# State sums of an SSD scan from split operands, and a group of small products cut in two

## The chip, the core and the metric

The kernel runs on one core of a Trainium2 chip. The time is what the device needs for one execution, in microseconds (us), as the median of several runs. TensorE (PE) multiplies, VectorE (DVE) and ScalarE (ACT) work elementwise, GpSimd (POOL) does small copies, and SyncE (SP) issues the DMAs.

## What is computed

Two layers of a hybrid decoder trunk for 512 prompt tokens and 8 x 8 sample tokens. Each layer projects the normed input to the inputs of three branches: an SSD (Mamba-2) scan of 16 heads, 8 retention heads, and pooling. A second projection takes their outputs back. The change touches two places of it, the sum that updates the SSD state after a chunk, and the product of the sample queries with the retention states. From the reference:

```python
def step(h, inp):                      # SSD, one chunk of 128 tokens
    ...
    y = jnp.einsum('btsg,btsgh,bsghp->btghp', scores, decay, xdt)
    y = y + jnp.einsum('btgn,bghpn->btghp', cc, h) * jnp.exp(cum)[..., None]
    last = cum[:, -1]
    w_end = jnp.exp(last[:, None] - cum)
    h_new = h * jnp.exp(last)[..., None, None] + jnp.einsum('bsgn,bsgh,bsghp->bghpn', bc, w_end, xdt)
...
def step(s, inp):                      # retention
    ...
    y = y + jnp.einsum('bthd,bhde->bthe', qc, s) * inner_decay[None, :, :, None]
```

All of it is in fp32.

## The kernel before

**Units.** A layer is a sequence of 60 units, u = 0 to 59. A unit is one projection of 128 output columns over all 576 tokens: 2 halves of 288 tokens x 8 steps k over the input. Each step is three fp32r products, high weights times high input, high times low, low times high (`products`, L554 to L556), so 48 products a unit. The operands are split for that: ScalarE copies the weights to fp32r (`high`, L942) and VectorE subtracts that copy from them (`split`, L1227), two units ahead. Everything else on TensorE stands between units, in program order, and runs in plain fp32.

**Order.** There is no planner. Each engine has its own loop over u, with the branch work written out by unit number, and semaphores between them. `project(u, between, at)` issues the 48 products and calls `between` after step number `at` (half * 8 + k). The SSD chunks t = 0 to 4 take units 26 to 35, two units a chunk; t = 4 is the sample tokens, and has no state sum. For chunks 0 to 3:

- TensorE, end of the even unit, `ssd_turn(t)`: transposes of x (L662) and B (L667) and the scores product. End of the odd unit, `ssd_y(t)`: first the state sums (L676), one fp32 product of 512 columns per group, then the 16 heads' outputs (L690, with L693 for the old state).
- VectorE, even unit, `ssd_1(t)` (L1380, L1381 makes `xdw`, L1383), the weight split (L1227), then `ssd_weights(t)` (L1392, twice), which multiplies the decays with the scores. Odd unit, `ssd_2(t)`: new state (L1422, L1425) and outputs (L1434), then `c_decay`. In units 28 and 30 a pooling chain (L1588 on) stands behind `ssd_weights`.
- ScalarE, even unit: the high half of the weights of unit u + 2, half of the decay's clamps (L1033), a copy of turned B to `btok` (L1119), the decay's exponentials (L1040), then the readout of the unit (L986 to L996).

**Waits.** Before L676 TensorE waits for `s_xdt` (`ssd_1`) and `s_bt` (L1119). Only before L690 it waits for `s_M` (`ssd_weights`):

```python
pe.wait_ge(*of(s_bt, t + 1))
if t < TILES - 1:
    for g in range(GROUPS):
        mm = pe.matmul(mb[:, g, :], btok[:, g, :], xdw[:, g * 512:(g + 1) * 512], start=True, stop=True)
    mm.then_inc(s_S, 1)
pe.wait_ge(*of(s_M, t + 1))
```

**Retention.** In unit 22 (`S_RST`) `ret_inter` runs after step 7: 64 fp32 products of 64 x 64 weights and 8 columns, L784, with one signal at the end (`rs_I`) for which VectorE waits in `ret_sample_y` (L1558); `ret_decayed` (L1569) follows there.

Of the kernel before, what the change touches and what calls it, by code (L numbers as in the profile page):

```python
# [8 lines left out]
F32 = mybir.dt.float32  # L9
# [4 lines left out]
P = 128  # L14
# [8 lines left out]
HEADS = 16  # L23
# [106 lines left out]
def trunk(nc: bass.Bass, a):  # L130
    with ExitStack() as ctx:
# [33 lines left out]
        decay = place("decay", [P, 2, HEADS, CH], at=work)  # L165
        cdec_t = place("c_decayed", [P, HEADS, CH], at=work + 4 * 4096)
        xdt = place("xdt", [P, HEADS * HD], at=work + 4 * 6144)
        xdw = place("xdt_to_end", [P, HEADS * HD], at=work + 4 * 7168)
        hT = place("ssm_state", [P, HEADS * HD], at=work + 4 * 8192)

# [18 lines left out]
        two_at = top[0]  # L189
        ssq = place("ssq", [P, TOK])  # L190
        rstd = place("rstd", [P, TOK])
        itok = place("sample_inter_tok", [P, HEADS * HD], at=two_at)
        tab = place("tab", [P, TAB_N])
        vec = place("vec", [P, V_N])
# [12 lines left out]
        gm = place("scores", [P, GROUPS, CH])  # L207
        btok = place("b_tok", [P, GROUPS, P])
        masked = top[0]
        bseq_ = place("b_tok_seq", [P, 2, GROUPS * P])  # L210
        el = place("exp_last", [P, HEADS])
        els = place("exp_last_sample", [P, HEADS, NB])
# [95 lines left out]
        sT = sem("ssd_turned", TILES)  # L308
        s_xdt = sem("ssd_xdt", TILES)
        s_bt = sem("ssd_b_tok", TILES)  # L310
        s_exp = sem("ssd_exps", TILES)
        s_row = sem("ssd_row_exps", TILES - 1)
        s_ec = sem("ssd_c_decayed", TILES - 2)
# [222 lines left out]
        def _(pe):  # L536
# [79 lines left out]
                        mm = products(0, half, k)  # L616
                mm.then_inc(proj, 1)

            def project(u, between=None, at=KT - 1):

                pe.wait_ge(*of(w_split, u + 1))
                o = u - U_OUT
                if u == 1:
                    pe.wait_ge(*of(x_new, 2 * OUT_CHUNKS, l - 1))
                elif o < 2:
                    pe.wait_ge(*of(evac, u - 1))
                else:
                    pe.wait_ge(*of(x_new, o - 1))
                for half in range(2):
                    for k in range(KT):  # L630
                        if half == 0 and u == EARLY:
                            pe.wait_ge(*of(h_lo, k + 1))
                        if half == 0 and o == 0:
                            pe.wait_ge(*of(mix_lo, k + 1))
                        if half == 0 and o == OUT_CHUNKS:
                            pe.wait_ge(*of(y_lo, k + 1))
                        mm = products(u, half, k)
                        if half * KT + k == at and between is not None:
                            between()
                mm.then_inc(proj, 1)  # L640

            def norm_sum(at):
# [27 lines left out]
            def ssd_y(t):  # L670
                n = rows(t)
                pe.wait_ge(*of(s_xdt, t + 1))
                pe.wait_ge(*of(s_bt, t + 1))
                if t < TILES - 1:
                    for g in range(GROUPS):
                        mm = pe.matmul(mb[:, g, :], btok[:, g, :], xdw[:, g * 512:(g + 1) * 512], start=True, stop=True)  # L676
                    mm.then_inc(s_S, 1)
                pe.wait_ge(*of(s_M, t + 1))
                inter = 0 < t < TILES - 1
                if inter:  # L680
                    pe.wait_ge(*of(s_ec, t))
                for j in range(PAIRS):
                    if t < TILES - 1:
                        dst = mb[:, 2 + j // 4, (j % 4) * P:(j % 4) * P + n]
                    else:
                        dst = mb[:, 2, j * SMP:(j + 1) * SMP]
                    for e in range(2):
                        h = 2 * j + e
                        r = slice(e * HD, (e + 1) * HD)
                        mm = pe.matmul(dst[r, :], xdt[0:n, h * HD:(h + 1) * HD], decay[0:n, t % 2, h, 0:n],  # L690
                                       start=True, stop=not inter)
                        if inter:
                            mm = pe.matmul(dst[r, :], hT[:, h * HD:(h + 1) * HD], cdec_t[:, h, :],  # L693
                                           start=False, stop=True)
                mm.then_inc(s_Y, 1)
# [77 lines left out]
                            mm = pe.matmul(mb[r, 1, j * HD:(j + 1) * HD], kw[:, c], vtok[:, c], start=True, stop=True)  # L773
                    mm.then_inc(r_S, 1)

            def ret_inter():

                pe.wait_ge(*of(r0_in, 16))
                for n in range(NB):
                    b = RET_SEQ_OF[n]  # L780
                    for j in range(RP):
                        for e in range(2):
                            r = slice(e * HD, (e + 1) * HD)
                            mm = pe.matmul(mb[r, 3 - e, j * SMP + b * NT:j * SMP + (b + 1) * NT],  # L784
                                           rs0[r, n // STRIPS, n % STRIPS, j, :], qd[r, j, b * NT:(b + 1) * NT],
                                           start=True, stop=True)
                mm.then_inc(rs_I, 1)

            def ret_sums(q):

# [77 lines left out]
            for l in range(DEPTH):  # L868
# [4 lines left out]
                for u in range(1, UNITS if l + 1 < DEPTH else UNITS - 2):  # L873
# [1 line left out]

                        pe.wait_ge(*of(pool_out, u - U_GPOOL - 1))
                    if u == S_RST:
                        project(u, ret_inter)
                    elif S_RST < u <= S_RST + 2:
                        project(u, lambda: ret_sums(u - S_RST - 1))  # L880
                    elif u == S_SST:

                        def beside():
                            pool_mm_(3)
                            ssd_inter(0)

                        project(u, beside)
                    elif u == S_SST + 1:
                        project(u, lambda: ssd_inter(1))
                        ssd_inter_turn()  # L890
                    elif u == S_SST + 2:
                        project(u, lambda: ssd_sums(0, 0))
                    elif u == S_SST + 3:
                        project(u, lambda: ssd_sums(0, 1), 2)
                        ssd_sums(1, 0)
                    elif u == S_SST + 4:
                        project(u, lambda: ssd_sums(1, 1), KT)
                    elif u == S_NORM + 2:
                        project(u, lambda: ssd_norm_sum(0))
                        ssd_norm_sum(1)  # L900
                    elif u == S_RN + 2:
                        project(u, lambda: (ret_norm_sum(2), ret_norm_sum(3)), KT + KT // 2)
                    elif U_GPOOL < u < U_GPOOL + 4 and (u - S_SSD) % 2 == 0:
                        project(u, lambda: pool_mm_(u - U_GPOOL - 1))
                    elif u > 1 or l:
                        project(u)
# [24 lines left out]
        def _(eng):  # L931
# [148 lines left out]
            for l in range(DEPTH):  # L1080
                for u in range(UNITS if l + 1 < DEPTH else UNITS - 2):
# [30 lines left out]
                    if even:  # L1112

                        t = (u - S_SSD) // 2
                        if t > 0:
                            ssd_clamp(t, 1, 2)
                            eng.wait_ge(*of(s_S, t))
                        eng.wait_ge(*of(sT, t + 1))
                        go(act(btok[:, :, :], mb[:, 3, 0:256].rearrange("p (g n) -> p g n", g=2), ACT.Copy),  # L1119
                           s_bt, t + 1)  # L1120
                        if t > 0:
                            ssd_decay(t)
                    if EARLY <= u < U_OUT:
# [32 lines left out]
                        ssd_clamp(0, u - S_RET, 4)  # L1156
                    if u == S_RET + 4:
                        ssd_decay(0)
                    if S_SSD <= u < S_SST - 1 and not even:
                        t = (u - S_SSD) // 2 + 1  # L1160
                        ssd_row_exps(t)
                        ssd_clamp(t, 0, 2)
# [55 lines left out]
        def _(eng):  # L1218
# [154 lines left out]
            def ssd_1(t):  # L1373
                n = rows(t)
                eng.wait_ge(*of(sT, t + 1))
                src = mb[:, 0:2, :].rearrange("p a (h d) -> p (a h) d", d=HD)
                dt_b = tokv[:, t, 32:48].unsqueeze(2).to_broadcast([P, HEADS, HD])
                dw_b = tokv[:, t, 64:80].unsqueeze(2).to_broadcast([P, HEADS, HD])
                settle()
                go(V.tensor_tensor(heads(xdt[:, :]), src, dt_b, ALU.mult))  # L1380
                go(V.tensor_tensor(heads(xdw[:, :]), src, dw_b, ALU.mult))  # L1381
                mask = (T("causal") if t < TILES - 1 else T("smask")[0:SMP, :])
                go(V.tensor_tensor(gm[0:n, :, 0:n], mb[0:n, 2, 0:256].rearrange("p (g n) -> p g n", g=2)[:, :, 0:n],  # L1383
                                   mask.unsqueeze(1).to_broadcast([n, GROUPS, n]), ALU.mult), s_xdt, t + 1)

            def ssd_weights(t):
                n = rows(t)
# [269 lines left out]
            for l in range(DEPTH):  # L1657
                for u in range(UNITS if l + 1 < DEPTH else UNITS - 2):
# [49 lines left out]
                    if S_SSD <= u < S_SST:  # L1708
                        t = (u - S_SSD) // 2
                        (ssd_weights if even else ssd_2)(t)  # L1710
                        if (u - S_SSD) % 2 == 1 and t + 1 < TILES - 1:
                            c_decay(t + 1)
                    if U_CONV <= u < U_POOL:
# [296 lines left out]
```

## Time and profile before

| | us |
|---|---|
| median of 3 runs | 954.91 (954.11 to 955.33) |
| the profiled execution | 958.53 |
| its span, first to last instruction | 956.7 |
| TensorE busy | 945.1 (99%) |
| VectorE busy | 679.9 (71%) |
| ScalarE busy | 423.7 (44%) |
| mean granted TensorE clock | 0.992 |

Read first which engine fills the span, then what it waits for, then its clock by stretches. A TensorE record lasts longer than its turn in the stream, since matmuls are pipelined: the distance between the starts of records is what a product costs. An fp32 product leaves two records, an fp32r product one.

### The profile page before, as it was taken

The page shows a single profiled execution, that of the slowest core. Times are in us where ns is not written, and L with a number is a line of the kernel's source. Part 1 is how long each engine was busy: PE and PEld are TensorE (multiplying, and loading weights), DVE is VectorE, ACT ScalarE, POOL GpSimd, SP SyncE. Part 2 cuts the span into 40 slices and gives each one's busy share as a digit, 9 for nine tenths or more (in the row PEclk, how much of TensorE's full clock was granted, in tenths as well). Part 3 has the DMA queues.
Part 4 walks back from the last instruction along what each step waited for, and adds up shares of the span by engine and source line. Part 5 has one row for each costly group of instructions (what it writes and reads, how often), then busy time and mean ns, then how long its engine had stood idle before and what let it go on. Part 6 is the DMA issues. An engine that isn't in the chain of part 4 may idle for free.

```text
span 956.7 us, 18777 instructions
## 1 busy us (share of the span) xinstructions
PE 945.1 (99%) x7942; PEld 898.9 (94%) x7942; DVE 679.9 (71%) x927; ACT 423.7 (44%) x710; POOL 43.5 (5%) x148
## 2 busy tenths in 40 slices
PE   8999999999999999999999999999999999999996
PEld 7899999999989889999999999999989988999996
DVE  6787778666995568664557877777679747786544
ACT  6432553235774145532334225532267632554243
POOL 0000101010010000000000001101101000000000
PEclk9999999899999999999999999998999999999999
DMA  7334222134234463323432442122433452562222
GB/s 277 105 116 140 69 66 67 51 111 155 91 106 158 152 223 127 131 91 111 132 128 66 135 143 67 46 67 53 159 105 101 138 200 66 221 209 67 76 80 100
DMA packets 38421, 112.56 MB, mean 118 GB/s; under 512 B 11104, under 2 KB 14048, under 8 KB 36928
## 3 DMA queue, kind: packets, MB, share of 16 engines
q1 hardware_dynamic: 38080, 110.46, 35.2%
q8 instruction: 63, 1.03, 0.5%
q0 software_dynamic: 256, 0.88, 0.3%
q14 instruction: 22, 0.18, 0.1%
HBM read 93.85 MB, written 17.47 MB: 116 GB/s over the span
## 4 chain that ended last, share of the span: by engine, by line
PE 90%; DVE 4%; ACT 4%; DMA 1%; issue 1%; SPq 0%; DVEq 0%; ACTq 0%
PE acc L554 26%; PE acc L556 25%; PE acc L555 25%; PE misc L690 1%; ACT decay L1033 1%; PE misc L676 1%; PE misc L743 1%; ACT w_hi L942 1%; PE misc L784 1%; PE misc L765 1%; DVE w_lo L1227 1%; PE acc L833 1%; PE misc L814 1%; ACT decay L1040 1%; PE misc L707 1%; DVE conv_out L1588 1%
## 5 line engine op out<-in xcount | busy, mean ns | idle before, releaser
L554 PE MATMUL acc<-hin,w_hi 128*128 128x288 f32 x1504 | 452.9, 301 | 0.3 <-DVE x L1673 0.3
L556 PE MATMUL acc<-hin,w_lo 128*128 128x288 f32 x1504 | 444.9, 296 | 0.0
L555 PE MATMUL acc<-hin,w_hi 128*128 128x288 f32 x1504 | 444.8, 296 | 0.0
L554 PEld LDWEIGHTS acc<-hin,w_hi 128*128 128x128 f32 x1504 | 284.2, 189 | 12.9 <-issue 11.3
L942 ACT ACTIVATE w_hi<-w_raw 128x1024 fp32r<-128x1024 f32 x119 | 125.8, 1057 | 379.9 <-PE acc L556 378.2
L555 PEld LDWEIGHTS acc<-hin,w_hi 128*128 128x128 f32 x1504 | 284.4, 189 | 0.4
L556 PEld LDWEIGHTS acc<-hin,w_lo 128*128 128x128 f32 x1504 | 284.1, 189 | 0.0
L1227 DVE TENSOR_TENSOR w_lo<-w_raw,w_hi 128x1024 fp32r<-128x1024 f32 x119 | 145.4, 1222 | 135.2 <-ACT w_hi L942 134.9
L554 PE MATMUL acc<-mix,w_hi 128*128 128x288 f32 x416 | 124.3, 299 | 1.3 <-DVE mix L1233 0.9
L556 PE MATMUL acc<-mix,w_lo 128*128 128x288 f32 x416 | 122.6, 295 | 0.0
L555 PE MATMUL acc<-mix,w_hi 128*128 128x288 f32 x416 | 122.5, 294 | 0.0
L554 PEld LDWEIGHTS acc<-mix,w_hi 128*128 128x128 f32 x416 | 78.0, 188 | 4.8 <-issue 3.5
L555 PEld LDWEIGHTS acc<-mix,w_hi 128*128 128x128 f32 x416 | 78.0, 188 | 0.3
L556 PEld LDWEIGHTS acc<-mix,w_lo 128*128 128x128 f32 x416 | 78.0, 188 | 0.0
L1333 DVE SCALAR_TENSOR_TENSOR conv_out<-halo,vec,conv_out 128x600 f32<-128x600 f32 x72 | 60.8, 844 | 2.5
L1033 ACT ACTIVATE decay<-decay,token_vecs 128x128 f32<-128x128 f32 (+1 forms) x160 | 47.8, 379 | 1.9
L1673 DVE TENSOR_TENSOR x<-x,acc 128x576 f32<-128x576 f32 x30 | 22.6, 754 | 28.4 <-PE acc L556 26.4
L946 ACT ACTIVATE mix<-x,vec 128x576 fp32r<-128x576 f32 x16 | 12.0, 770 | 38.7 <-DVE x L1673 34.5
L690 PE MATMUL misc<-decay,xdt 128*64 128x128 f32 (+1 forms) x320 | 27.3, 266 | 0.0
L960 ACT ACTIVATE tmp<-x 128x576 f32<-128x576 f32 x22 | 14.8, 679 | 25.5 <-DVE x L1673 12.2
L690 PEld LDWEIGHTS misc<-decay,xdt 128*64 128x64 f32 (+1 forms) x320 | 19.5, 136 | 6.8 <-issue 6.8
L1380 DVE TENSOR_TENSOR xdt<-misc,token_vecs 128x1024 f32<-128x1024 f32 x10 | 12.2, 1225 | 18.1 <-PE misc L667 17.8
(218 smaller groups left out, 1052.6 us busy)
## 6 DMA issues: line engine op xcount, KB each, us to landing
w_raw<-in_w SPq DMA_DIRECT2D x119, 512.0 KB, 3.7
decay<-cum_rows SPq DMA_DIRECT2D x8, 1024.0 KB, 6.2
h<-in_ssm SPq DMA_DIRECT2D x16, 512.0 KB, 6.7
out_ssm_s<-h SPq DMA_DIRECT2D x16, 512.0 KB, 6.0
x<-in_x SPq DMA_DIRECT2D x8, 576.0 KB, 6.3
x_kept<-x SPq DMA_DIRECT2D x4, 576.0 KB, 2.8
x<-x_kept SPq DMA_DIRECT2D x4, 576.0 KB, 5.8
out_y<-x SPq DMA_DIRECT2D x8, 288.0 KB, 2.3
```

Source lines behind the costliest of these rows:

```text
L554: pe.matmul(out, wh, hi, start=k == 0, stop=False)
L555: pe.matmul(out, wh, lo, start=False, stop=False)
L556: return pe.matmul(out, wl, hi, start=False, stop=k == KT - 1)
L690: mm = pe.matmul(dst[r, :], xdt[0:n, h * HD:(h + 1) * HD], decay[0:n, t % 2, h, 0:n], start=True, stop=not inter)
L942: go(act(w_hi[:, unit % 2, :, :], w_raw[:, unit % RAW, :, :], ACT.Copy), w_hid, unit + 1, 0)
L946: go(act(raw_h(0, j), x[:, j, :], ACT.Copy, scale=vec[:, V_NW + j:V_NW + j + 1]), p_hi, j + 1, at)
L960: go(act(tmp[:, j % 2, :], x[:, j, :], ACT.Square), sqd, j + 1, at)
L1033: go(act(m, m, ACT.Relu, scale=-1.0, bias=tokv[0:n, t, h:h + 1]))
L1227: go(V.tensor_tensor(w_lo[:, unit % 2, :, :], w_raw[:, unit % RAW, :, :], w_hi[:, unit % 2, :, :].bitcast(F32), ALU.subtract), w_split, un ...
L1333: ins = V.scalar_tensor_tensor(out=o, in0=h[:, c:c + CVO], scalar=w[c], in1=o, op0=ALU.mult, op1=ALU.add)
L1380: go(V.tensor_tensor(heads(xdt[:, :]), src, dt_b, ALU.mult))
L1673: go(V.tensor_tensor(halves(x[:, m, :]), halves(x[:, m, :]), acc_of(whole(l, u)), ALU.add), x_new, o + 1)
```

## The change

The state sums of chunks 0 to 3 become three fp32r products per group, from split operands. The high half of turned B is written by the ScalarE copy that made `btok` before, now of type fp32r. The high half of `xdw` is a new ScalarE copy of 1024 elements, behind the readout of the even unit. The low halves are two VectorE subtractions in a new `ssd_low`, called behind `ssd_weights`. TensorE waits for a new semaphore, `s_xlo`, before the sums. Separately, `ret_inter` is cut into two calls of 32 products, after steps 2 and 9 of unit 22; the signal comes after the second.

```diff
@@ ssd_y
                 if t < TILES - 1:
+                    pe.wait_ge(*of(s_xlo, t + 1))
                     for g in range(GROUPS):
-                        mm = pe.matmul(mb[:, g, :], btok[:, g, :], xdw[:, g * 512:(g + 1) * 512], start=True, stop=True)
+                        b, c = slice(g * P, (g + 1) * P), slice(g * 512, (g + 1) * 512)
+                        pe.matmul(mb[:, g, :], btok_2[:, 0, b], xdw_hi[:, c], start=True, stop=False)
+                        pe.matmul(mb[:, g, :], btok_2[:, 0, b], xdw_lo[:, c], start=False, stop=False)
+                        mm = pe.matmul(mb[:, g, :], btok_2[:, 1, b], xdw_hi[:, c], start=False, stop=True)
                     mm.then_inc(s_S, 1)
@@ ret_inter
-            def ret_inter():
+            def ret_inter(part):
 
                 pe.wait_ge(*of(r0_in, 16))
-                for n in range(NB):
+                for n in range(STRIPS * part, STRIPS * (part + 1)):
...
-                mm.then_inc(rs_I, 1)
+                if part:
+                    mm.then_inc(rs_I, 1)
@@ TensorE's loop
                     if u == S_RST:
-                        project(u, ret_inter)
+                        project(u, lambda: ret_inter(0), 2, lambda: ret_inter(1), KT + 1)
@@ ScalarE's loop
-                        go(act(btok[:, :, :], mb[:, 3, 0:256].rearrange("p (g n) -> p g n", g=2), ACT.Copy),
-                           s_bt, t + 1)
+                        if t < TILES - 1:
+                            go(act(btok_2[:, 0, :], mb[:, 3, 0:256], ACT.Copy), s_bt, t + 1)
+                        else:
+                            go(act(btok[:, :, :], mb[:, 3, 0:256].rearrange("p (g n) -> p g n", g=2), ACT.Copy),
+                               s_bt, t + 1)
...
+                    if even and t < TILES - 1:
+                        eng.wait_ge(*of(s_xdt, t + 1))
+                        go(act(xdw_hi[:, :], xdw[:, :], ACT.Copy), s_xhi, t + 1)
@@ VectorE
+            def ssd_low(t):
+
+                eng.wait_ge(*of(s_bt, t + 1))
+                go(V.tensor_tensor(btok_2[:, 1, :], mb[:, 3, 0:256], btok_2[:, 0, :].bitcast(F32), ALU.subtract))
+                eng.wait_ge(*of(s_xhi, t + 1))
+                settle()
+                go(V.tensor_tensor(xdw_lo[:, :], xdw[:, :], xdw_hi[:, :].bitcast(F32), ALU.subtract), s_xlo, t + 1)
...
                         (ssd_weights if even else ssd_2)(t)
+                        if even and t < TILES - 1:
+                            ssd_low(t)
```

The new tiles lie in memory that is free in those units: `xdw_lo` over `xdw` itself, `xdw_hi` over the norm's two work tiles, `btok_2` over `b_tok_seq`.

## Rows read from the trace of the kernel before

**Rows 1.** The page: busy time of the engines.
```profile
PE 945.1 (99%) x7942; PEld 898.9 (94%) x7942; DVE 679.9 (71%) x927; ACT 423.7 (44%) x710; POOL 43.5 (5%) x148
```

**Rows 2.** Waits of TensorE, the longest: in total us, times, longest us.
```profile
PE misc L867 <- DVE pad_eps L1640: 1.7, 1, 1.7
```

**Rows 3.** TensorE by windows: us, busy (records), clock, DMA share, GB/s.
```profile
180.00:190.00 10.00, 10.00 (x152) 0.66 0.19 61
...
183.00:184.00 1.00, 1.00 (x26) 0.54 0.00 0
...
650.00:651.00 1.00, 1.00 (x36) 0.85 0.06 13
```

**Rows 4.** TensorE's timeline at the retention products: start, duration, then the instruction.
```profile
179.67 0.29 PE L555 MATMUL acc<-hin,w_hi 128*128 128x288 f32 x1
179.80 0.29 PE L556 MATMUL acc<-hin,w_lo 128*128 128x288 f32 x1
180.03 4.50 PE L784 MATMUL misc<-q_decayed,ret 64*64 64x8 f32 x128
...
184.86 0.44 PE L555 MATMUL acc<-hin,w_hi 128*128 128x288 f32 x1
185.10 0.44 PE L556 MATMUL acc<-hin,w_lo 128*128 128x288 f32 x1
...
647.94 4.75 PE L784 MATMUL misc<-q_decayed,ret 64*64 64x8 f32 x128
```

**Rows 5.** TensorE's timeline at the state sums of chunk 0: all four records, then the last alone.
```profile
226.18 1.88 PE L676 MATMUL misc<-xdt_to_end,b_tok 128*128 128x512 f32 x4
...
227.47 0.59 PE L676 MATMUL misc<-xdt_to_end,b_tok 128*128 128x512 f32 x1
```

**Rows 6.** VectorE's timeline in the unit before them.
```profile
222.30 0.41 DVE L1383 TENSOR_TENSOR scores<-misc,tab 128x256 f32<-128x256 f32 x1
222.63 1.22 DVE L1227 TENSOR_TENSOR w_lo<-w_raw,w_hi 128x1024 fp32r<-128x1024 f32 x1
223.95 2.36 DVE L1392 TENSOR_TENSOR decay<-decay,scores 128x1024 f32<-128x1024 f32 x2
```

**Rows 7.** Timeline of all engines at chunk 1, some lines.
```profile
242.45 2.36 DVE L1392 TENSOR_TENSOR decay<-decay,scores 128x1024 f32<-128x1024 f32 x2 [0.56 <-ACT decay L1040]
...
243.73 0.65 ACT L991 ACTIVATE qk<-acc 128x576 f32<-128x576 f32 x1
244.12 0.32 PEld L676 LDWEIGHTS misc<-xdt_to_end,b_tok 128*128 128x128 f32 x2
244.24 1.88 PE L676 MATMUL misc<-xdt_to_end,b_tok 128*128 128x512 f32 x4
244.50 1.06 ACT L942 ACTIVATE w_hi<-w_raw 128x1024 fp32r<-128x1024 f32 x1
```

**Rows 8.** The same view at chunk 3.
```profile
282.31 2.36 DVE L1392 TENSOR_TENSOR decay<-decay,scores 128x1024 f32<-128x1024 f32 x2
283.48 0.65 ACT L996 ACTIVATE tmp<-acc 128x576 f32<-128x576 f32 x1
...
285.32 1.88 PE L676 MATMUL misc<-xdt_to_end,b_tok 128*128 128x512 f32 x4
```

**Rows 9.** The same view at chunk 1 of the second layer.
```profile
711.65 0.65 ACT L991 ACTIVATE qk<-acc 128x576 f32<-128x576 f32 x1
...
712.16 1.88 PE L676 MATMUL misc<-xdt_to_end,b_tok 128*128 128x512 f32 x4
```

**Rows 10.** VectorE behind the retention products; VectorE and TensorE at the turn of chunk 3.
```profile
191.53 1.22 DVE L1227 TENSOR_TENSOR w_lo<-w_raw,w_hi 128x1024 fp32r<-128x1024 f32 x1 [3.70 <-ACT w_hi L942]
...
273.67 2.16 DVE L1434 SCALAR_TENSOR_TENSOR xbc<-xbc,vec,misc 128x128 f32<-128x128 f32 x8
...
276.08 1.03 PE L662 MATMUL misc<-tab,xbc 128*128 128x128 f32 x8
```

**Rows 11.** TensorE by windows, behind its last product.
```profile
951.10:954.40 3.30, 0.00 (x0) 1.00 0.87 307
```

More of the change, by code:

```diff
@@ L167, in trunk @@
         xdt = place("xdt", [P, HEADS * HD], at=work + 4 * 6144)
+        xdw_lo = place("xdt_to_end_low", [P, HEADS * HD], F32R, at=work + 4 * 7168)
         xdw = place("xdt_to_end", [P, HEADS * HD], at=work + 4 * 7168)
@@ L191, in trunk @@
         rstd = place("rstd", [P, TOK])
+        xdw_hi = place("xdt_to_end_high", [P, HEADS * HD], F32R, at=two_at)
         itok = place("sample_inter_tok", [P, HEADS * HD], at=two_at)
@@ L209, in trunk @@
         masked = top[0]
+        btok_2 = place("b_tok_high_low", [P, 2, GROUPS * P], F32R, at=masked)
         bseq_ = place("b_tok_seq", [P, 2, GROUPS * P])
@@ L310, in trunk @@
         s_bt = sem("ssd_b_tok", TILES)
+        s_xhi = sem("ssd_to_end_high", TILES - 1)
+        s_xlo = sem("ssd_to_end_split", TILES - 1)
         s_exp = sem("ssd_exps", TILES)
@@ L617, in project_again, with project @@
                 mm.then_inc(proj, 1)
-            def project(u, between=None, at=KT - 1):
+            def project(u, between=None, at=KT - 1, then=None, then_at=KT):
                 pe.wait_ge(*of(w_split, u + 1))
@@ L639, in project @@
                             between()
+                        if half * KT + k == then_at and then is not None:
+                            then()
                 mm.then_inc(proj, 1)
```

## The prediction

> **What bounds the kernel now.** I read the page first: TensorE is busy for 945.1 us, 99% of the span [rows 1]. Then the waits of TensorE: the longest is 1.7 us, at the start, and all others are under 1 us, none of them in chunk work [rows 2]. So TensorE bounds every stage, and whatever TensorE does or waits for is on the path that sets the end. Third, its clock by stretches: the mean is 0.66 in 180 to 190 us. Windows of 1 us show where it goes from the higher of its two levels (1.00, 2.4 GHz) to the lower (0.50, 1.2 GHz): 0.54 in 183 to 184 us is a fall at 183.1, and in the second layer 0.85 in 650 to 651 us is one at 650.7 [rows 3]. The two layers show nothing else of the kind. What TensorE did before each fall is the timeline's: 128 records of 8 columns (the retention sample products) for 4.5 us [rows 4]. Last, for each chunk, when TensorE reaches the state sums and when VectorE and ScalarE are done [rows 5 to 9]: VectorE is closer to being late than the busy shares tell.
>
> **Part 1, the state sums on TensorE (L676).** Now one chunk takes two fp32 products, in four records. The first starts at 226.18, the fourth at 227.47, so they follow each other every 1.29 / 3 = 0.43 us, 1.72 us in all [rows 5]. Afterwards there are six fp32r products of 512 columns; the trace has none of that size. The fp32r products of 288 columns come every 0.13 us (a whole unit of 48 gives 0.133), and every 0.24 at the low clock [rows 4]. 0.24 us for 288 columns at 1.2 GHz is one column a cycle, so at 2.4 GHz a product is 0.120 plus 0.013 us. With a fixed extra, 512 columns take 0.213 + 0.013 = 0.226, six take 1.36; in proportion 0.236, six take 1.42. I take the first: the extra is absent at the low clock, where the columns take twice as long, so it doesn't look proportional. Gain per chunk 0.36 (0.30) us, times 8 chunks (4 in each of 2 layers): **-2.9 us** (-2.4). A loss is excluded: it would need 0.29 a product, over twice the 288-column row. The change of tile shape on the way to L690 stays as it is. The records show two records for an fp32 product, each of 0.43 us for 512 columns, two cycles of 2.4 GHz a column, so four in all. The Trainium skill ("FP8 and Floating Point Precision", section TensorE Precision Notes) says that true FP32 takes four passes; the trace agrees. The skill's "TensorE: Matmul & The Clock Gate" (section Back-to-back issue gap) has 2.5 ns over the columns' time where the rows have 13; by it, as an estimate, six would take 1.30 us and the gain be 3.4 us; the rows decide.
>
> **Part 2, what TensorE now waits for.** The sums need both halves of the split. ScalarE copies the high half (1024 elements a partition) after its readout; VectorE subtracts twice, and *after* its two score products (L1392). Until now the scores were needed only at L690, 1.8 us after TensorE reached the sums. That cover is taken away, and two more VectorE instructions are put before the same point. Prices: the subtraction of 1024 has a twin, L1227, 1.22 us; the one of 256 from PSUM is like L1383, 0.41 (it follows at 0.33) [rows 6]; the copy of 1024 is like L942, 1.06 us [rows 7]. A released engine starts 0.05 us later, and a product starts 0.12 us after its weight load [rows 7]; between independent instructions of ScalarE or VectorE lies an overlap of about 0.09 us [rows 6, 7].
> Chunk 0: scores end 223.95 + 2.36 = 226.31; small subtraction to 226.64; large one 226.68 to 227.90; TensorE starts at 228.07 instead of 226.18 [rows 5, 6]: wait 1.89 us. The copy is done earlier: ScalarE only reads out in this unit.
> Chunk 1: here ScalarE is last. Its Silu readout ends at 243.73 + 0.65 = 244.38, the copy runs 244.29 to 245.35, the large subtraction 245.40 to 246.62, TensorE starts 246.79 instead of 244.24: 2.55 us [rows 7]. (On VectorE alone, with scores to 244.81, it would be some 0.4 less.)
> Chunk 2 repeats chunk 1, with the same operations at the same distances: 2.55 us.
> Chunk 3: a pool product (L833) makes TensorE arrive later. Silu from 283.48, copy to 285.10, subtraction to 286.37, start 286.54 instead of 285.32: 1.22 us [rows 8].
> Together 8.21 us a layer. Layer 2 has the same distances (Silu 711.65, arrival 712.16, against 243.73 and 244.24) [rows 7, 9]: **+16.4 us**. Lower bound, VectorE alone, small subtraction 0.33, no refill of the array: about 1.6 + 2.0 + 2.0 + 0.6 = 6.2 a layer, 12.4. Upper bound, 0.3 us more for each chunk in handing over: 18.8.
> Queued behind the new instructions: on VectorE the pool chains of chunks 1 and 2, the next weight split and the state update (L1434 ends 273.67 + 2.16 = 275.83, just before TensorE's turn of chunk 3 at 276.08) [rows 10]. It shifts by some 1.7 us, TensorE by 2.55 - 0.36 = 2.2, so its margin grows from 0.25 to about 0.7: no second wait. On ScalarE the next high half of the weights comes up to 0.9 us later, and TensorE isn't there either. Cost of both: 0.
>
> **Part 3, the retention products in two parts.** If the clock stays up, the low stretches go. Layer 1: the mean of 0.66 means 0.34 / 0.5 x 10 = 6.8 us at the low level, from 183.1 to 189.9. From 184.5, where the small products end, one product comes every 0.24 instead of 0.133 us: 5.4 / 0.24 = 22.5 products, 2.4 us. In the 1.4 us before, the small products themselves ran slower, x26 in 183 to 184 against the mean of 128 / 4.4 = 29, about 0.45 us [rows 3, 4]. In layer 2 the fall comes 0.3 us earlier in the group and the group is 0.25 us longer; I take the same 2.85 us. Together **-5.7 us**. Cost: one more change of tile shape into and out of the small products, about 0.1 us each way (as 179.80 to 180.03 where 0.13 is usual) [rows 4]: +0.4 us. The products end some 0.9 us later, at index 9 instead of 7 of the unit, and what VectorE does behind them is followed by an idle of 3.70 us [rows 10]: 0.
>
> **Sum.** 16.4 - 2.9 - 5.7 + 0.4 = +8.2 us. The profiled execution took 958.53 us, 1.8 over its span: it would become 966.7. It lies 3.6 above the median of 954.91, and my forecast is for the median: **963.1 us**.
>
> **Rivals.** *B, the clock falls in the new waits.* Before, TensorE had no pause over 1.7 us in its stream. A pause of 2.5 us, four of them in 8 chunks, could send it to the low level, where it stayed 6.8 us [rows 3]. That costs 6.8 x (1 - 0.133 / 0.24) = 3.0 us for each fall; one to four falls give 966.1 to 975. Against it: behind its last product TensorE did nothing from 951.1 to 954.4, and the clock was still at 1.00 [rows 11]. For it: it fell although TensorE was never idle [rows 3, 4]. The Trainium skill (the clock page above, section Why this matters for your kernels) blames drops on idle gaps between bursts; the two falls here had no gap, so the trace shows that it takes less, and the page's rule gives this rival, not the forecast.
> *C, the split doesn't hold the clock.* Each part still has 64 records, nearly 2 us of work that hardly fills the array. If both layers still fall, the 5.7 us stay: 968.8. For the split speaks that both falls came 2.8 to 3.1 us after the start of the group (183.1 against 180.03, 650.7 against 647.94) [rows 3, 4], longer than a part.
> *D, faster.* The gains of 8.2 us win if the eight waits sum to less than 8.2, 1.0 us each. That happens if the work ahead of the sums is shorter by half: since the scores alone end 0.13 us (chunk 0) and 0.57 us (chunk 1) after TensorE's arrival and 0.65 before it (chunk 3) [rows 5 to 8], what comes behind them would have to cost 0.6 us instead of 1.6. With free subtractions the waits would be some 0.3 + 0.7 + 0.7 us a layer, 3.4 in all, and the time 954.9 + 3.4 - 8.2 = 950.1. Against it stands the twin instruction at 1.22 us.
>
> **How the numbers follow.** Forecast 50%, B 27%, C 13%, D 5%, and 5% for times just around the kernel before. The forecast's own bounds: 954.9 + 12.4 - 2.9 - 5.8 + 0.2 = 958.8, and 954.9 + 18.8 - 2.4 - 5.5 + 0.6 = 966.4. The range has to take in C and up to two or three falls of B: 958.5 to 971. A measurement can tell about 0.2% (1.9 us) from no change. Slower 92%, same 4%, faster 4%.
>
> **What would show it.** A row "L676-line products <- VectorE xdt_to_end" among TensorE's waits, 16 us in 8 times, 1.9, 2.5, 2.5 and 1.2 long; fp32r products of 512 columns every 0.226 us; the clock at 1.00 in the small products, now in two groups of some 1.9 us; L1434 and the turns without a wait. Wrong would be: waits of half that length (then D), a clock of 0.5 behind the sums (B) or in the retention unit (C), or a wait at the turn of chunk 3.

## The result and the profile after

| | us |
|---|---|
| before, median | 955.12 |
| after, median | 972.63 (971.29 to 973.40) |
| ratio | 1.0172, 95% interval 1.0150 to 1.0193 |
| profiled execution after, and its span | 973.24, 971.5 |
| before, profiled execution and span | 958.53, 956.7 |

The change makes the kernel 17.5 us slower, by the profiled executions 14.7 us. I had forecast 8.2 us, and the range ended at 971.

The waits of TensorE in the kernel after (in total us, times, longest us), which answer [rows 2]:

```profile
PE misc L685 <- DVE xdt_to_end_low L1410: 14.9, 8, 2.3
PE misc L879 <- DVE pad_eps L1666: 1.7, 1, 1.7
```

One line is new: the sums (L685) wait 8 times for the large subtraction. The pauses of the engine are 1.8 us in chunk 0, 2.3 in chunks 1 and 2 and 1.0 in chunk 3 of both layers. The timeline at chunk 1, the answer to [rows 7]:

```profile
244.06 0.65 ACT L1003 ACTIVATE qk<-acc 128x576 f32<-128x576 f32 x1
244.60 1.05 ACT L1176 ACTIVATE xdt_to_end_high<-xdt_to_end 128x1024 fp32r<-128x1024 f32 x1
245.05 0.42 DVE L1407 TENSOR_TENSOR b_tok_high_low<-misc,b_tok_high_low 128x256 fp32r<-128x256 f32 x1
...
245.69 1.23 DVE L1410 TENSOR_TENSOR xdt_to_end_low<-xdt_to_end,xdt_to_end_high 128x1024 fp32r<-128x1024 f32 x1 [0.21 <-ACT xdt_to_end_high L1176]
...
247.06 0.47 PE L685 MATMUL misc<-xdt_to_end_high,b_tok_high_low 128*128 128x512 f32 x1 [2.34 <-DVE xdt_to_end_low L1410]
```

It is the chain of the prediction, link by link: readout, copy on ScalarE, a small gap of VectorE until it is done, the subtraction, TensorE 0.14 us later. The idle number, 2.34, counts from the modelled end of the record before; the product before started at 244.43 and would have been followed in 0.13 us, so the sums start 2.50 us late. Measured in that way the four chunks of a layer wait 1.94, 2.50, 2.51 and 1.16 us, 8.1 us, where I had 1.89, 2.55, 2.55 and 1.22.

TensorE by windows (us, busy, clock, DMA share, GB/s) in the kernel after, the answer to [rows 3]:

```profile
180.00:190.00 10.00, 10.00 (x125) 1.00 0.18 56
220.00:230.00 10.00, 8.22 (x64) 0.83 0.33 106
240.00:250.00 10.00, 7.66 (x67) 1.00 0.17 52
265.00:275.00 10.00, 7.66 (x69) 0.83 0.18 54
650.00:660.00 10.00, 10.00 (x181) 1.00 0.27 69
715.00:725.00 10.00, 7.66 (x54) 0.83 0.19 53
740.00:750.00 10.00, 7.66 (x66) 0.83 0.18 52
```

In the retention unit (180 to 190, and 650 to 660) the clock now stays at 1.00. But it is at 0.83 in four stretches, each around one of the eight pauses: 0.17 / 0.5 of 10 us is 3.4 us at the lower level, 1.2 GHz. Windows of 0.5 us put the four falls at 225.7, 270.1, 720.6 and 744.5; the pauses beside them ended at 225.17, 269.17, 720.95 and 744.46. So two falls come 0.5 and 0.9 us behind a pause, one at its end, and one, in chunk 1 of layer 2, in the pause itself, before any of the sums' products had run:

```profile
720.00:720.50 0.50, 0.00 (x0) 1.00 0.00 0
720.50:721.00 0.50, 0.05 (x1) 0.64 0.00 0
```

What a fall does to the products shows in chunk 0:

```profile
225.17 0.47 PE L685 MATMUL misc<-xdt_to_end_high,b_tok_high_low 128*128 128x512 f32 x1 [1.78 <-DVE xdt_to_end_low L1410]
225.48 0.42 PE L686 MATMUL misc<-xdt_to_end_low,b_tok_high_low 128*128 128x512 f32 x1
225.71 0.62 PE L687 MATMUL misc<-xdt_to_end_high,b_tok_high_low 128*128 128x512 f32 x1
226.13 0.63 PE L685 MATMUL misc<-xdt_to_end_high,b_tok_high_low 128*128 128x512 f32 x1
226.55 0.63 PE L686 MATMUL misc<-xdt_to_end_low,b_tok_high_low 128*128 128x512 f32 x1
```

The distance from one to the next goes from 0.23 to 0.42 us.

Setting the starts of the same projection units side by side in both traces gives where the 14.7 us arose: the retention unit -2.7 us in each layer; the chunks +3.25, +2.24, +3.85, +0.90 in layer 1 and +1.69, +3.63, +3.79, +0.93 in layer 2; at the start of the kernel -0.2. Chunk 0 costs 3.25 with a fall of the clock and 1.69 without, and chunk 1 costs 3.63 with one and 2.24 without: a fall costs 1.4 to 1.6 us.

### The profile page after: what moved, and what is told of

It reads as the page before. It is cut to its first block, busy times and chain, and to the rows that moved or that the text cites. A ratio compares the mean times of both kernels' runs of the same rounds, so it can differ in the third digit from the quotient of the medians.

```text
span 971.5 us, 18841 instructions
## 1 busy us (share of the span) xinstructions
PE 945.7 (97%) x7958; PEld 901.2 (93%) x7958; DVE 692.3 (71%) x943; ACT 430.9 (44%) x718; POOL 41.3 (4%) x148
## 4 chain that ended last, share of the span: by engine, by line
PE 89%; ACT 6%; DVE 4%; issue 1%; ACTq 0%; DVEq 0%
PE acc L559 25%; PE acc L561 24%; PE acc L560 24%; PE misc L701 2%; ACT decay L1045 1%; ACT w_hi L954 1%; ACT decay L1052 1%; PE misc L704 1%; PE misc L754 1%; DVE xdt_to_end_low L1410 1%; PE misc L776 1%; DVE w_lo L1245 1%; PE misc L795 1%; PE misc L826 1%; PE misc L718 1%; PE misc L685 1%
## 5 line engine op out<-in xcount | busy, mean ns | idle before, releaser
L972 ACT ACTIVATE tmp<-x 128x576 f32<-128x576 f32 x22 | 14.9, 680 | 25.3 <-DVE x L1699 12.2
```

The lines of the kernel that those rows point to most:

```text
L972: go(act(tmp[:, j % 2, :], x[:, j, :], ACT.Square), sqd, j + 1, at)
```

## The experiments

Two questions: are the falls made by the pauses, and what is the retention split worth in a usual execution? Several executions of the kernel before had taken 954 to 955 us, the profiled one 958.5. Every kernel below was timed beside the kernel before on the same chip; the median of that one was 955.57, 955.49 and 955.27 us in the three rounds, within 0.3 us of each other.

**The kernel before, once more.** No edit.

> The kernel before, unchanged, once more. Its profiled execution took 958.5 us, its other executions 954 to 955. Theory 1 (the falls of the clock differ from execution to execution, and the profiled one had long ones): executions near 954 to 955 show a mean clock of 0.994 to 0.996, those near 958 one of 0.992; a profile at 955 has low stretches of 3.4 us in the retention unit in place of 6.8. Theory 2 (the profiled execution was slower for another reason): the clock is 0.992 in all of them.

Ten executions took from 954.06 to 958.68 us, and the time follows the mean clock: 954.06 and 954.21 at 0.996, 955.37 and 955.90 at 0.994, 957.03 at 0.993, 958.19 to 958.68 at 0.990 or 0.991. The profile fell on the fastest one. Its TensorE windows:

```profile
180.00:190.00 10.00, 10.00 (x164) 0.83 0.20 63
645.00:655.00 10.00, 10.00 (x175) 1.00 0.26 67
```

The same program loses 3.4 us of high clock in layer 1 and none in layer 2 here, 6.8 in each in the execution on which I had built. Theory 1 holds: the clock in this unit falls differently from execution to execution. (The executions at 955.4 and 955.9 had a clock of 0.994, as expected; that more of them lay at 958 than I had thought changes nothing of it.)

**The retention split alone.**

```diff
@@ kernel before
-                for n in range(NB):
+                for n in range(STRIPS * part, STRIPS * (part + 1)):
...
-                        project(u, ret_inter)
+                        project(u, lambda: ret_inter(0), 2, lambda: ret_inter(1), KT + 1)
```

> The kernel before with the retention products in two parts, and nothing else. The clock should stay up in unit 22 of both layers. Against the profiled execution of before (span 956.7) each layer should save 2.7 us there, a span of 951.2. Theory 1 (a usual execution of before loses less to the clock than the profiled one): the median is 1.5 to 3 us below that of before. Theory 2: it is 5.5 us below.

953.00 us (952.73 to 953.84) against 955.57, ratio 0.9965 (0.9953 to 0.9977): a small gain, clear of the noise. All twelve executions lie within 1.1 us and their clock is 0.997 or more. The products and the windows:

```profile
177.91 2.04 PE L786 MATMUL misc<-q_decayed,ret 64*64 64x8 f32 x64
182.84 2.04 PE L786 MATMUL misc<-q_decayed,ret 64*64 64x8 f32 x64
```
```profile
180.00:190.00 10.00, 10.00 (x124) 1.00 0.16 51
645.00:655.00 10.00, 10.00 (x128) 1.00 0.20 62
```

The span is 951.2, as expected to the tenth. Where the clock had not fallen in the kernel before (layer 2 of the execution above), the split costs 0.28 us. So it is worth 5.6 us against the profiled execution of before and 2.6 in the median, as theory 1 has it.

**The split sums alone**, with both retention parts issued after step 7 again.

```diff
@@ kernel after
-                        project(u, lambda: ret_inter(0), 2, lambda: ret_inter(1), KT + 1)
+                        project(u, lambda: (ret_inter(0), ret_inter(1)))
```

> The changed kernel with the retention products in one part again, so the split sums alone. The waits before the sums stay (1.9, 2.5, 2.5, 1.2 us, 16.2 us in all), the clock falls in unit 22 again. If the two parts of the change add up: 2 to 5.5 us slower than the changed kernel, 974 to 978 us. If the falls behind the sums come only by the phase that the two parts bring with them: none here, and then 970 us or less.

974.42 us (974.20 to 974.62), ratio 1.0190 (1.0169 to 1.0212). That is 1.8 us over the changed kernel, at the lower edge of what was expected if the parts add up, and far from the 970 of the other theory. The waits are the same eight, 14.9 us by the waits view, and the trace shows low stretches of 3.4 us behind chunk 2 of both layers besides those of the retention unit (6.8 us in layer 1, 3.4 in layer 2).

**The waits without the fp32r products.** The low halves are made and waited for, but left out of the sums.

```diff
@@ kernel after, ssd_y
                         b, c = slice(g * P, (g + 1) * P), slice(g * 512, (g + 1) * 512)
-                        pe.matmul(mb[:, g, :], btok_2[:, 0, b], xdw_hi[:, c], start=True, stop=False)
-                        pe.matmul(mb[:, g, :], btok_2[:, 0, b], xdw_lo[:, c], start=False, stop=False)
-                        mm = pe.matmul(mb[:, g, :], btok_2[:, 1, b], xdw_hi[:, c], start=False, stop=True)
+                        mm = pe.matmul(mb[:, g, :], btok_2[:, 0, b].bitcast(F32), xdw_hi[:, c].bitcast(F32), start=True, stop=True)
```

> The changed kernel with one fp32 product per group in place of three fp32r, on the high halves alone (the low halves are made and waited for, but not multiplied). Against the changed kernel each chunk's sums take 1.72 in place of 1.36 us. My theory (the pauses make the clock fall, whatever product follows): pauses of 1.8 and 2.3 us as before, three to four falls of 3.4 us behind them, time 972.6 + 2.9 = 975.5 us (974 to 977). Rival (the denser fp32r products bring the falls): no fall, time 969 to 970.

974.52 us (972.83 to 976.50), ratio 1.0199 (1.0174 to 1.0225). The pauses are the same, and the clock falls for 3.4 us behind four of them, those of chunks 1 and 2 in both layers. The rival, that denser products bring the falls, is out: plain fp32 products have them too. And two of the four falls begin within the pause. The sums of chunk 2 started at 270.25 here, and TensorE had stood idle since 267.91:

```profile
267.91:269.90 1.99, 0.00 (x0) 1.00 0.18 74
269.90:270.25 0.35, 0.00 (x0) 0.62 0.00 0
```

**The products without the waits.** The two terms with low halves are left out, so the sums are not the right ones; only the time is of use.

```diff
@@ kernel after
-                    pe.wait_ge(*of(s_xlo, t + 1))
...
-                        pe.matmul(mb[:, g, :], btok_2[:, 0, b], xdw_lo[:, c], start=False, stop=False)
-                        mm = pe.matmul(mb[:, g, :], btok_2[:, 1, b], xdw_hi[:, c], start=False, stop=True)
+                        pe.matmul(mb[:, g, :], btok_2[:, 0, b], xdw_hi[:, c], start=False, stop=False)
+                        mm = pe.matmul(mb[:, g, :], btok_2[:, 0, b], xdw_hi[:, c], start=False, stop=True)
...
-                go(V.tensor_tensor(heads(xdw[:, :]), src, dw_b, ALU.mult))
+                xd = xdw_hi if t < TILES - 1 else xdw
+                go(V.tensor_tensor(heads(xd[:, :]), src, dw_b, ALU.mult))
```

> The changed kernel without the low halves: VectorE writes the high half directly, the copy on ScalarE, both subtractions and the new wait are gone, and the three fp32r products all take high halves (the terms with low halves are left out). It measures the products alone, on top of the retention split (953.0 us). My theory: 1.36 in place of 1.72 us a chunk, no pause, no fall: 950.1 us. If the products cost in proportion to columns: 950.6. If fp32r gives nothing here: 953.0. If a fall comes by the denser products: 952 or more.

951.07 us (950.59 to 951.75), ratio 0.9949 (0.9929 to 0.9970), 1.9 us below the split alone. No wait in the chunks, clock 0.997 to 0.999. TensorE's timeline in chunk 0:

```profile
223.40 0.40 PE L684 MATMUL misc<-xdt_to_end_high,b_tok_high_low 128*128 128x512 f32 x1
223.63 0.39 PE L685 MATMUL misc<-xdt_to_end_high,b_tok_high_low 128*128 128x512 f32 x1
223.86 0.40 PE L686 MATMUL misc<-xdt_to_end_high,b_tok_high_low 128*128 128x512 f32 x1
...
224.56 0.40 PE L686 MATMUL misc<-xdt_to_end_high,b_tok_high_low 128*128 128x512 f32 x1
```

The last of six starts at 224.56, 1.16 us after the first: 0.232 us each. That lies between the 0.226 that I took and the 0.236 in proportion to the columns. Each chunk gains 0.32 us, 2.6 in all. Of that, 0.24 us a layer is given back at the turn of chunk 3, which then has to wait for VectorE:

```profile
270.25 2.16 DVE L1457 SCALAR_TENSOR_TENSOR xbc<-xbc,vec,misc 128x128 f32<-128x128 f32 x8
...
272.55 1.06 PE L669 MATMUL misc<-tab,xbc 128*128 128x128 f32 x8
```

L1457 ends at 272.41. This is the 0.25 us margin of [rows 10]: with the products alone TensorE arrives 1 us earlier and VectorE doesn't. So with VectorE's order as it is, the split sums could bring about 2 us here, even if their operands cost nothing.

**Shorter pauses.** ScalarE's copy ahead of its readout, the small subtraction ahead of the scores.

```diff
@@ kernel after, ScalarE
+                    if even and t < TILES - 1:
+                        eng.wait_ge(*of(s_xdt, t + 1))
+                        go(act(xdw_hi[:, :], xdw[:, :], ACT.Copy), s_xhi, t + 1)
                     if EARLY <= u < U_OUT:
                         read_out(u)
@@ VectorE
+                        if even and t < TILES - 1:
+                            ssd_low_b(t)
                         (ssd_weights if even else ssd_2)(t)
```

> The changed kernel with ScalarE's copy ahead of its readout and VectorE's small subtraction ahead of the scores. My theory (chunks 1 and 2 wait for ScalarE's copy, then for the large subtraction): start to start 1.9, 1.9 in place of 2.5 there, chunk 0 as before (1.9), chunk 3 1.0; 3 us less of waits, and fewer falls: 968 us (966 to 970). If every fall needs a pause of over 2 us: no fall in any execution and 966 or less. If the copy was not what chunks 1 and 2 waited for: 972 as before.

969.83 us (965.03 to 970.96), ratio 1.0143 (1.0119 to 1.0167). The profile:

```profile
PE misc L685 <- DVE xdt_to_end_low L1413: 11.1, 6, 1.9
PE acc L845 <- ACT tmp L1008: 2.2, 2, 1.1
```

Chunks 1 and 2 now pause for 1.90 instead of 2.34 us, so the copy was what they waited for. In chunk 3 the wait moved: TensorE stands before the pool product (L845), for a readout that now comes behind the copy. The six executions also show what the clock costs: one had no fall (clock 0.998) and took 965.03, the profiled one; four had 0.993 and took 969.5 to 970.2, one 0.991 and 970.96. It is the same program, 5 us apart. A mean clock 0.005 lower is about three falls of 3.4 us (an estimate, as these five weren't profiled, and it doesn't say where they fell). That a pause under 2 us can be enough, the trace of the kernel after shows at chunk 0: 1.78 us, and a fall 0.5 us behind it.

**Outputs first, sums behind them.**

```diff
@@ kernel after, ssd_y
-                if t < TILES - 1:
-                    pe.wait_ge(*of(s_xlo, t + 1))
...
-                    mm.then_inc(s_S, 1)
                 pe.wait_ge(*of(s_M, t + 1))
...
                 mm.then_inc(s_Y, 1)
+                if t < TILES - 1:
+                    pe.wait_ge(*of(s_xlo, t + 1))
...
+                    mm.then_inc(s_S, 1)
```

VectorE's small subtraction stands ahead of the scores (not in this excerpt).

> The changed kernel, but TensorE computes the chunk's outputs first and the state sums behind them; VectorE's small subtraction stands ahead of the scores, the large one stays behind them. The wait that is left is that for the scores: 0.6, 0.7, 0.7, 0 us a chunk, 4 us in all in place of 16.2. My theory (waits for the low half, plus falls of the clock behind pauses of 2.5 us): no fall is left, and the time is 952 us (950 to 954), faster than before. Rival (the falls come from the denser or shorter fp32r products themselves, not from the pauses): the clock still falls behind the sums, and the time is 956 to 958. Rival (VectorE is just late by the sum of its added work, and the turns of the next chunk wait instead): new waits before L669, time near 960.

957.86 us (957.68 to 958.40), ratio 1.0024 (1.0012 to 1.0036). The mean clock is 0.997 or more in all twelve executions, as my theory wanted, and the sums don't wait. But the time is 6 us too long for it. TensorE waits for the scores for 4.7 us (L693), up to 1.2 each, and anew at the turns of chunks 2 and 3:

```profile
PE misc L693 <- DVE decay L1421: 4.7, 6, 1.2
...
PE misc L669 <- DVE xbc L1463: 1.7, 4, 0.7
```

With the 951.07 of the products alone these two waits make 957.5. The third theory is partly right: VectorE is late by its added work, and that moves to the next place where TensorE needs it.

**The same with the old-state products ahead.** They don't need the scores and cover the wait for them. Beside the diff of the last experiment and the one below, ScalarE's copy stands ahead of its readout, and in chunk 0 VectorE's weight split stands behind the low halves (both not in the excerpt).

```diff
@@ kernel after, ssd_y
+                if inter:
+                    pe.wait_ge(*of(s_ec, t))
+                    for j in range(PAIRS):
+                        for e in range(2):
...
+                            pe.matmul(dst_of(j)[r, :], hT[:, h * HD:(h + 1) * HD], cdec_t[:, h, :],
+                                      start=j % 4 == 0, stop=False, skip_group_check=True)
+                pe.wait_ge(*of(s_M, t + 1))
```

> Built to win: like e3_outputs_first, but the products with the old state come first (they don't need the scores), then the others, then the sums; in chunk 0 the weight split of VectorE stands behind the low halves; ScalarE's copy ahead of its readout. The wait for the scores is covered by 0.85 us of products in chunks 1 to 3, and in chunk 0 by the moved split. My theory: no pause at the scores, 1.5 us of waits at the turns of chunks 2 and 3 (VectorE's queue is full there), -2.9 us for the products: 951 to 952.5 us, against 953.0 for the retention split alone. Rival (VectorE's work for the low halves is worth more than 2.9 us wherever it stands): 953 to 958 us.

957.79 us (957.33 to 958.36), ratio 1.0026 (1.0014 to 1.0037), so the rival was right. The waits for the scores are gone, those at the turns have grown, and one before the pool product is new:

```profile
PE misc L670 <- DVE xbc L1469: 5.0, 4, 2.0
PE acc L851 <- ACT tmp L1014: 2.2, 2, 1.1
```

VectorE has no gap of over 0.1 us from 258 to 287 us in this trace. In chunks 1 and 2 it has no room for 1.5 us more; wherever TensorE's order puts the wait, it comes. The 2.2 us at L851 are another matter: they come from the copy ahead of the readout, on ScalarE. The same order with the copy behind the readout was not run; taking these 2.2 us off gives 955.6 as an estimate, still above the 953.0 of the retention split alone. (In 3 of the 12 executions the clock was 0.994 or 0.996; the longest pause of the profiled one, whose clock stayed up, is 1.97 us.)

**The large subtraction on GpSimd.** ScalarE's copy stands behind its readout again.

```diff
@@ the last kernel, GpSimd in place of VectorE
+            def ssd_low(t):
+
+                eng.wait_ge(*of(s_xhi, t + 1))
+                settle()
+                go(G.tensor_tensor(xdw_lo[:, :], xdw[:, :], xdw_hi[:, :].bitcast(F32), ALU.subtract), s_xlo, t + 1)
```

> e7_sums_last with the large subtraction on GpSimd (44 us busy in 957) in place of VectorE, and ScalarE's copy behind its readout again. VectorE keeps only the small subtraction (0.33 us a chunk). My theory (in e7 the turns of chunks 2 and 3 waited 2.5 us a layer because VectorE's queue had no gap left in these chunks): those waits go to 0.3 us or less, the pool products no longer wait for ScalarE (1.1 us a layer), and the time is 953.0 - 2.6 + 0.5 = 951 us (950.5 to 952), below the retention split alone. Rival (GpSimd needs over 3 us for 1024 elements): the sums wait for it, 953 to 957 us, with waits of L705-line products on GpSimd.

964.60 us (963.83 to 966.10), ratio 1.0103 (1.0086 to 1.0120): neither theory. GpSimd is fast enough, 2.4 to 2.7 us, but look at VectorE beside it:

```profile
221.04 2.72 POOL L1856 TENSOR_TENSOR xdt_to_end_low<-xdt_to_end,xdt_to_end_high 128x1024 fp32r<-128x1024 f32 x1 [2.26 <-ACT xdt_to_end_high L1182]
```
```profile
221.44 3.41 DVE L1421 TENSOR_TENSOR decay<-decay,scores 128x1024 f32<-128x1024 f32 x1
```

The second score product takes 3.41 us in place of 1.22; it ends 1.1 us after GpSimd's. The pool chains of chunks 1 and 2 are hit in the same way. An addition beside GpSimd's subtraction of chunk 2, then the same in the trace of the experiment before:

```profile
264.83 3.07 DVE L1617 TENSOR_TENSOR conv_out<-halo 128x710 f32<-128x710 f32 x1
...
264.36 0.90 DVE L1623 TENSOR_TENSOR conv_out<-halo 128x710 f32<-128x710 f32 x1
```

So in chunks 0 to 2 VectorE is rid of 1.2 us of work and pays 2.1 to 2.2 us for it in other instructions. TensorE waits for the scores of chunk 0 for 1.5 us a layer (3.0 in all), and the turns of chunks 2 and 3 wait for VectorE up to 2.8 us (7.8 us in all), with two falls of the clock behind the pauses in this trace. The Trainium skill ("SBUF — State Buffer", section Who interferes with whom) has this rule: a VectorE instruction with two SBUF inputs contends with a GpSimd instruction that reads SBUF, and the ports that they share are an exclusive lock. The trace agrees: each of the three VectorE stretches beside a GpSimd subtraction is 2.1 to 2.2 us longer, and GpSimd's take 2.4 to 2.7 us.

None of the versions of the split sums run here that multiply both halves beats the kernel before. The retention split alone does, with 953.0 us.

## Why the prediction was wrong

Two terms of the sum failed: the clock behind the new waits, put at nothing, measured about 6 us; and the retention split, booked at -5.3 us, measured -2.6 in the median. The waits themselves, the mechanism that makes the change a loss, were right.

- **What bounds, and that the sums wait**: right. 16.4 us were forecast, 16.2 came, in the sizes and with the last link named for chunk 1 (the copy, then the large subtraction). (The aside that VectorE alone would save 0.4 us in chunk 1 doesn't follow from its terms, which give 0.2; only the lower bound used it.)
- **The six fp32r products**: -2.6 where I had -2.9. I took the extra over the columns as fixed; at 0.232 us a product the measured cost lies about midway between my 0.226 and the rejected 0.236.
- **The retention split**: -2.7 us a layer against the profiled execution, -5.5 in all with its cost, where I had -5.7 + 0.4. This is right against that execution. The step that failed is in the paragraph on the sum: I made the sum against one profiled execution and carried its difference over to the median. That execution had the longest low stretches, and it lay 3.6 us above the median for just this reason; the number stood in my text, and I didn't ask what it was made of. In the median the split is worth 2.6 us, so about 3 us of my gain weren't there to be had.
- **The clock behind the new pauses**: this is the step that cost most. I had it as a rival (B) at 27%, priced at 3.0 us a fall, and left it out of the forecast. It happened four times in the profiled execution, and the clock of the other three, 0.991 to 0.994 where a trace without such a fall has 0.998, says that they had falls too. A fall here lasts 3.4 us and costs 1.5, half of my price, since I had taken the 6.8 us of the retention unit. Four of them, 6 us, are the larger part of the error. The evidence that I set against the rival was a clock of 1.00 behind TensorE's last product [rows 11]. It misled me twice. The window ended just before the clock fell: the last product had ended at 949.9, the row ends at 954.40, and the next stretch of the same trace has the fall:

```profile
954.40:955.00 0.60, 0.00 (x0) 0.58 1.07 373
```

And it was one draw. In the eleven traces of this case the clock falls from 1.8 to 4.6 us after the last product; that trace has the longest time of all, and in the kernel after it is 1.8 us (964.6 to 966.4). A pause of 2.5 us lies inside that spread.
- **The range** ended at 971 because it took in only part of B. Put together from the experiments, against the median: +16.2 (waits) - 2.6 (products) - 2.6 (retention split) + 6 (falls) = +17, and 17.5 were measured.
- **What is late next**: right for this kernel, no turn waits. With the pauses taken away, the turn of chunk 3 is what comes next, and its margin of 0.25 us is all there is; I had seen the margin and not what it says of any repair.

The new falls stand behind or in idle gaps of 1.8 to 2.3 us, the old ones behind none: both kinds are in these traces. The Trainium skill ("TensorE: Matmul & The Clock Gate", section Why this matters for your kernels) names idle gaps between bursts as what brings throughput drops, but longer gaps than any pause of these sums; so its rule covers neither kind, and it did not give rival B as I wrote. How many falls an execution has is not settled by the program alone, since the same kernel had none and several; what sets it, these runs don't tell.

## What to carry to other kernels

A faster form of a product that needs prepared operands is paid on the engines that prepare them: here 2.6 us of TensorE's time against 1.5 us more of VectorE's in each chunk, in a stretch where VectorE was nearly full (24.0 of the 26 us from 250 to 276 in the kernel before) though its mean was 71%. Before a wait is put ahead of a step, look when each of its sources is ready in that very stage, and whether work behind it in the queue was the cover for another wait. And where a program's time varies with the clock, a profile is one draw: compare its low stretches with the spread of the executions before a gain from it is booked.

## What was not expected of the hardware

- A pause of TensorE of 1.8 to 2.3 us in otherwise dense work brings the clock down for 3.4 us, often but not always: behind or in four of six such pauses in the traces of the kernel after and of the waits without the fp32r products, two of six with the split sums alone, none of six in the profiled execution of the shorter pauses. No fall stood beside the pauses of about 1.0 us in chunk 3. At the end of the kernel, with no more work, it stayed up for 1.8 to 4.6 us.
- The 64 fp32 products of 8 columns bring it down in one group (3.9 us long while the clock stays up, 4.5 or 4.75 with a fall in it), for 3.4 or 6.8 us or not at all. In the trace with two groups of 2.0 us and 2.8 us of dense work between them there is no fall, and that kernel's 12 executions lie within 1.1 us.
- A GpSimd subtraction of 128 x 1024 from SBUF, 2.7 us, made a VectorE product of the same size take 3.41 in place of 1.22 us.
